# HGRN decay levels: split order on ScalarE and VectorE, query product ahead of the predicated copies, and the place of slab 12

## The chip, the cores and the metric

The kernel runs on one core of a Trainium2 chip. The metric is the device time of one execution in microseconds, the median of three. Both kernels compute the same thing on the same inputs.

## What is computed

A two-block model on 256 tokens with a model width of 1024, batch 1. The first block is a Mamba-2 mixer and a product-key expert layer; the second is an HGRN2 mixer, a gated convolutional FFN, windowed attention, and a second FFN. All of it is in float32. The part around the change is the HGRN2 mixer, which the reference writes by chunks of 32 tokens:

```python
def hgrn2_mixer(x, w_in, lower_bound, out_norm, w_out):
    q, f, i, g = jnp.split(x @ w_in, 4, axis=-1)
    q = jax.nn.silu(q) * HG_EXPAND ** -0.5
    forget = lower_bound + (1.0 - lower_bound) * jax.nn.sigmoid(f)
    logf = jnp.log(forget)
    k = 1.0 - forget
    o = hgrn2_chunked(heads(q), heads(k), heads(i), heads(logf))
    o = rms_norm(o, out_norm) * jax.nn.silu(heads(g))
    return o.reshape(b_, s_, D_MODEL) @ w_out
```

Inside `hgrn2_chunked` the score of a query t and an earlier key s is the sum over 128 features of q[t] k[s] exp(cum[t] - cum[s]), where cum is the running sum of logf. There are 8 heads.

## The kernel before

**Weights.** All weights pass through the core once, as a stream of 524 slabs of 128 x 1024 float32 (512 KB each), in a ring of 4 slots. SyncE loads a slab into `raw`. ScalarE copies it to `whi` (rounded to fp32r, the function `split_hi`, line 239), VectorE makes `wlo = raw - whi` (`split_lo`, line 247), and TensorE multiplies with both parts. A slab's `hi` waits until TensorE is done with the slab four places earlier in the ring (`slabs_done`), its `lo` waits for its `hi`, and the load of a slab waits for the `lo` of the slab four earlier.

**The HGRN stage.** Features f and q are projected first. Then 16 slabs, called 0 to 15 here, carry the projections of i and g, 12 matmuls of 512 columns each (`up_wide`, lines 326 to 328). Slabs 0 to 7 fill banks 0 to 3 with v, ScalarE copies these banks out (line 2098), and slabs 8 to 15 fill them again with the gate. In the text, "split k" is the pair `hi(k)`, `lo(k)` that prepares slab k+3: `hi(k)` may start once TensorE has finished slab k-1.

Between the slabs stand the nine *levels* that build the 256 x 256 decayed scores without ever forming an exponential that overflows. Level 8 is the diagonal, level 0 is the cross block between the two halves of the sequence, levels 1 to 7 have spans 64, 32 and so on down to 1. They run in the order 8, 0, 1, ..., 7. For a level x from 0 to 7:

- VectorE, `differences(x)`, here d(x): two subtractions of cum against the reference token of each block (lines 2180 and 2182).
- ScalarE, `level_exp(x)`, here e(x): two exponentials, query side and key side (lines 2063 and 2064). It waits for d(x).
- VectorE, `q_side(x)`, here q(x): the product of the query side with q (line 2217). It waits for the first half of e(x).
- TensorE, `level(x)`, here L(x): 16 float32 matmuls (8 for level 0) into banks 4 to 7; each shows as two records in the profile (line 1948; level 0 is line 1939). It waits for q(x), for e(x), and, bank by bank, for the take of the level before it.
- VectorE, `take(x)`, here t(x): four predicated copies, one per bank, that keep the level's own blocks (line 2233; for level 0 two plain copies, line 2226).

The buffers of d, e and q are two, so d(x) waits for L(x-2). After level 7 and slab 13 come the read-out (line 1970 on), slabs 14 and 15, the normalisation, the gate, and the output projection. Read-out waits for t(7).

**What sets the order.** No scheduler: each engine's queue is written out by hand, and each engine works its queue strictly as written. Two tables rule it, `LEVEL_ORDER` and `AFTER`, which says which slabs TensorE multiplies behind which level. ScalarE and VectorE derive the places of their splits from the same table. ScalarE's rule is the loop

```python
while done <= max(AFTER[x], default=0) + 1 and done < 14:
    slot_free(done)
    done += 1
if x + 2 < 8:
    level_exp(x + 2)
```

where `slot_free(k)` is `hi(k)`, with the four copies of v ahead of it for k = 8. So `hi` runs ahead of the exponentials of the same turn.

Of the kernel before, what the change touches and what calls it, by code (L numbers as in the profile page):

```python
# [131 lines left out]
def build(nc, t):  # L132
    ctx = ExitStack()
    with ctx:
# [21 lines left out]
        def V(name, i=0, n=1):  # L156
            o = VEC[name][0]
            if isinstance(i, int):
                return vec[:, o + i:o + i + n]
            return vec[:, bass.ds(i + o, n)]  # L160
# [36 lines left out]
        def s(name):  # L197

            if name not in S:
                S[name] = sem(name)  # L200
            return S[name]
# [31 lines left out]
        def split_hi(act, n0, i, r, U):  # L233
            if isinstance(i, int) and at(n0, i, r, U) >= N_SLABS:
                return
            q = slot(n0, r)
            act.wait_ge(raw_ready[q], (rounds(n0, i, r, U) + 1) * 16)
            act.wait_ge(slabs_done, at(n0, i, r, U) + 1)
            nc.scalar.activation(whi[:, q * 1024:(q + 1) * 1024], raw[:, q * 1024:(q + 1) * 1024],  # L239
                                 ACT.Copy).then_inc(hi_ready, 1)  # L240

        def split_lo(dve, n0, i, r, U):
            if isinstance(i, int) and at(n0, i, r, U) >= N_SLABS:
                return
            q = slot(n0, r)
            dve.wait_ge(hi_ready, at(n0, i, r, U) + 1)
            nc.vector.tensor_tensor(wlo[:, q * 1024:(q + 1) * 1024], raw[:, q * 1024:(q + 1) * 1024],  # L247
                                    whi[:, q * 1024:(q + 1) * 1024].bitcast(F32), ALU.subtract)\
                .then_inc(lo_ready, 1)
# [1656 lines left out]


        LEVEL_ORDER = (8, 0, 1, 2, 3, 4, 5, 6, 7)
        AFTER = {8: (2,), 0: (3,), 1: (4, 5), 2: (6, 7), 3: (8, 9), 4: (10,), 5: (11, 12), 6: (), 7: (13,)}
        PLACE_OF = {x: at for at, x in enumerate(LEVEL_ORDER)}  # L1910

        def span_of(x):
            return ((P,) + LEVELS[:-1])[x]

        def pe_hgrn(pe):
# [4 lines left out]
            def wide(k):  # L1920
                up_wide(pe, N_HG + 16 + k // 8 * 8, k % 8, s("v_out") if k == 8 else None)

            def level(x):

                before = LEVEL_ORDER[PLACE_OF[x] - 1] if PLACE_OF[x] else None
                if x < 8:
                    pe.wait_ge(s("qk_q"), x + 1)
                    pe.wait_ge(s("e_k"), x + 1)

                def bank_free(b):  # L1930
                    if before is not None:
                        pe.wait_ge(s("level_out"), 4 * PLACE_OF[x] - 4 + (4 if before == 0 else b + 1))

                qk = QK[x % 2]
                if x == 0:
                    for hd in range(HG_H):
                        if hd % 4 == 0:
                            bank_free(hd // 4)
                        nc.tensor.matmul(bank[4 + hd // 4][:, (hd % 4) * P:(hd % 4 + 1) * P],
                                         qk[:, hd * SEQ:hd * SEQ + P], qk[:, hd * SEQ + P:(hd + 1) * SEQ],  # L1940
                                         start=True, stop=True).then_inc(s("level_mm"), 2)
                    return
                for hc in range(2 * HG_H):
                    if hc % 4 == 0:
                        bank_free(hc // 4)
                    q = slice(hc * P, (hc + 1) * P)
                    a, b = (KK[:, q], QQ[:, q]) if x == 8 else (qk[:, q], qk[:, q])
                    nc.tensor.matmul(bank[4 + hc // 4][:, (hc % 4) * P:(hc % 4 + 1) * P], a, b,  # L1948
                                     start=True, stop=True).then_inc(s("level_mm"), 1)
# [8 lines left out]
            for x in LEVEL_ORDER:  # L1958
                level(x)
                for k in AFTER[x]:  # L1960
                    wide(k)
# [62 lines left out]
        def act_hgrn(act, chain):  # L2024
# [31 lines left out]
            def split(k):  # L2056
                split_hi(act, N_HG + 16 + k + AHEAD, 0, 0, 4)

            def level_exp(x):
                m = span_of(x)  # L2060
                act.wait_ge(s("dcum"), 2 * x + 2)
                e = QK[x % 2].rearrange("p (b w) -> p b w", w=2 * m)
                nc.scalar.activation(e[:, :, m:2 * m], e[:, :, m:2 * m], ACT.Exp).then_inc(s("e_q"), 1)
                nc.scalar.activation(e[:, :, 0:m], e[:, :, 0:m], ACT.Exp, scale=-1.0).then_inc(s("e_k"), 1)
# [29 lines left out]
            def slot_free(k):  # L2094
                if k == 8:
                    act.wait_ge(slabs_done, N_HG + 16 + 8 + RING)
                    for b in range(4):
                        nc.scalar.activation(VT[:, b * 512:(b + 1) * 512], bank[b][:, :], ACT.Copy)\
                            .then_inc(s("v_out"), 1)
                split(k)  # L2100
# [2 lines left out]
            split(0)  # L2103
            split(1)
            level_exp(1)
            done = 2
            for x in LEVEL_ORDER:
                while done <= max(AFTER[x], default=0) + 1 and done < 14:
                    slot_free(done)
                    done += 1  # L2110
                if x + 2 < 8:
                    level_exp(x + 2)
            split(14)
            nc.scalar.activation(tiny[:, 28:29], V("one"), ACT.Sqrt)
            squares(0)
            squares(1)
# [11 lines left out]
        def dve_hgrn(dve, chain):  # L2128
# [42 lines left out]
            def differences(x):  # L2171

                m = span_of(x)
                if x >= 2:
                    dve.wait_ge(s("level_mm"), 16 * (PLACE_OF[x - 2] + 1))
                e = QK[x % 2].rearrange("p (b w) -> p b w", w=2 * m)
                c3 = CUM.rearrange("p (b w) -> p b w", w=2 * m)
                k3 = CKN.rearrange("p (b w) -> p b w", w=2 * m)
                ref = c3[:, :, m - 1:m].to_broadcast([P, HG_H * SEQ // (2 * m), m])
                nc.vector.tensor_tensor(e[:, :, m:2 * m], c3[:, :, m:2 * m], ref, ALU.subtract)\  # L2180
                    .then_inc(s("dcum"), 1)
                nc.vector.tensor_tensor(e[:, :, 0:m], k3[:, :, 0:m], ref, ALU.subtract).then_inc(s("dcum"), 1)
# [26 lines left out]
            def split(k):  # L2209
                split_lo(dve, N_HG + 16 + k + AHEAD, 0, 0, 4)  # L2210

            def q_side(x):
                m = span_of(x)
                dve.wait_ge(s("e_q"), x + 1)
                e = QK[x % 2].rearrange("p (b w) -> p b w", w=2 * m)
                q3 = QQ.rearrange("p (b w) -> p b w", w=2 * m)
                nc.vector.tensor_tensor(e[:, :, m:2 * m], e[:, :, m:2 * m], q3[:, :, m:2 * m], ALU.mult)\
                    .then_inc(s("qk_q"), 1)

            def take(x):  # L2220

                at = PLACE_OF[x]
                if x == 0:
                    for b in range(2):
                        dve.wait_ge(s("level_mm"), 16 * at + 8 * (b + 1))
                        nc.vector.tensor_copy(CR[:, b * 512:(b + 1) * 512], bank[4 + b][:, :])\
                            .then_inc(s("level_out"), 2)
                    return
                for b in range(4):
                    dve.wait_ge(s("level_mm"), 16 * at + 4 * (b + 1))  # L2230
                    if at:
                        dve.wait_ge(s("level_out"), 4 * (at - 1) + b + 1)
                    nc.vector.copy_predicated(
                        PP[:, b * 512:(b + 1) * 512].rearrange("p (c t) -> p c t", t=P),
                        MASK[:, (x - 1) * P:x * P].bitcast(U32).unsqueeze(1).to_broadcast([P, 4, P]),
                        bank[4 + b][:, :].rearrange("p (c t) -> p c t", t=P)).then_inc(s("level_out"), 1)
# [6 lines left out]
            q_side(0)  # L2243
            split(1)
            for x in LEVEL_ORDER:
                if AFTER[x]:
                    split(AFTER[x][0])
                take(x)
                if x < 7:
                    q_side(x + 1)  # L2250
                if x + 2 < 8:
                    differences(x + 2)
                for k in AFTER[x][1:]:
                    split(k)
            split(14)

            def sums(half):
                for tt in range(TT):
# [461 lines left out]
        def act_block2(act, chain):  # L2720
            act_hgrn(act, chain)
            act_ffn(act, 0)
            act_attn(act, chain)
            act_ffn(act, 1)
            turn_act(act, T_OUT)
# [185 lines left out]
```

## Time and profile before

| what | value |
|---|---|
| median of 3 runs | 1718.12 us (1717.89 to 1719.43) |
| profiled execution | 1720.73 us |
| its span, first to last instruction | 1718.9 us |
| TensorE busy | 1672.3 us, 97% |
| VectorE busy | 1285.4 us, 75% |
| ScalarE busy | 1032.1 us, 60% |
| level stage, first level matmul to end of slab 13 | 1140.67 to 1209.36 us |

The span is what the trace covers; the profiled execution's own time has 1.83 us around it. Timeline rows give the start in microseconds from the span's start, the duration, engine, line, operation, output and input, and in brackets how long the engine sat idle before and which instruction released it. On VectorE and ScalarE a row's duration includes its tail, which overlaps the next instruction's start, so the step from start to start is what an instruction costs the queue.

### The profile page before, as it was taken

To read this page: it belongs to the slowest core of one execution; us is meant where nothing else is said; L and a number is where in the kernel's file an instruction comes from. 1 tells how busy PE (TensorE), PEld (TensorE's weight loads), DVE (VectorE), ACT (ScalarE), POOL (GpSimd) and SP (SyncE) were. 2 spreads that over 40 slices of the span, in tenths; PEclk is the share of its full clock that TensorE was granted. 3 is DMA by queue.
4 is the path that set the end of the run, shared out by engine and by line. 5 is a ranking of instruction groups with operands and counts; after the bars stand their busy time and mean duration, and the time that the engine had idled before them with its cause. 6 is when DMAs were issued, how large, how long until landed. Compare 5 with 4: busy or idle time off the path is not lost.

```text
span 1718.9 us, 34380 instructions
## 1 busy us (share of the span) xinstructions
PE 1672.3 (97%) x10835; PEld 1507.6 (88%) x10835; DVE 1285.4 (75%) x2361; ACT 1032.1 (60%) x1629; POOL 110.4 (6%) x101
## 2 busy tenths in 40 slices
PE   7999999999999999999999999999999998999998
PEld 6998889999999999988888888898888888778886
DVE  6876773799967777777777777789677777877776
ACT  7656554667556666655445445764576567666665
POOL 0014300344100000000000000100000000000000
PEclk9999999999999999999999999999999999999999
DMA  5543356577765555477787777543346554246563
GB/s 200 165 148 101 108 176 216 172 225 229 231 213 169 179 171 177 165 233 241 243 268 242 243 242 239 174 148 98 123 160 192 191 192 140 90 143 207 183 190 116
DMA packets 113261, 315.62 MB, mean 184 GB/s; under 512 B 12624, under 2 KB 44752, under 8 KB 112688
## 3 DMA queue, kind: packets, MB, share of 16 engines
q1 hardware_dynamic: 112352, 310.83, 55.9%
q0 software_dynamic: 848, 4.00, 0.7%
q8 instruction: 35, 0.57, 0.1%
q14 instruction: 26, 0.21, 0.0%
HBM read 296.43 MB, written 18.35 MB: 183 GB/s over the span
## 4 chain that ended last, share of the span: by engine, by line
PE 89%; DVE 5%; ACT 4%; issue 2%; DMA 1%; ACTq 0%; DVEq 0%; SPq 0%
PE bank L269 11%; PE bank L270 11%; PE bank L271 11%; PE bank L334 10%; PE bank L335 10%; PE bank L336 10%; PE bank L290 9%; PE bank L294 5%; PE bank L1496 3%; PE bank L1948 1%; DVE wlo L247 1%; ACT whi L239 1%; PE bank L326 1%; PE bank L328 1%; PE bank L327 1%
## 5 line engine op out<-in xcount | busy, mean ns | idle before, releaser
L247 DVE TENSOR_TENSOR wlo<-raw,whi 128x1024 fp32r<-128x1024 f32 x499 | 613.9, 1233 | 145.5 <-ACT whi L239 135.8
L239 ACT ACTIVATE whi<-raw 128x1024 fp32r<-128x1024 f32 x524 | 550.5, 1052 | 42.4 <-PE bank L328 36.0
L269 PE MATMUL bank<-x,whi 128*128 128x256 f32 (+1 forms) x1728 | 507.5, 294 | 5.2 <-DVE arena L897 1.7
L271 PE MATMUL bank<-x,wlo 128*128 128x256 f32 (+1 forms) x1728 | 491.7, 285 | 0.0
L270 PE MATMUL bank<-x,whi 128*128 128x256 f32 (+1 forms) x1728 | 491.4, 284 | 0.0
L269 PEld LDWEIGHTS bank<-x,whi 128*128 128x128 f32 x1728 | 331.3, 192 | 10.1 <-issue 8.1
L270 PEld LDWEIGHTS bank<-x,whi 128*128 128x128 f32 x1728 | 331.8, 192 | 0.1
L271 PEld LDWEIGHTS bank<-x,wlo 128*128 128x128 f32 x1728 | 331.0, 192 | 0.0
L334 PE MATMUL bank<-whi,yhi 128*128 128x512 f32 x816 | 319.5, 392 | 3.3 <-DVE ylo L716 1.9
L335 PE MATMUL bank<-wlo,yhi 128*128 128x512 f32 x816 | 318.2, 390 | 0.0
L336 PE MATMUL bank<-whi,ylo 128*128 128x512 f32 x816 | 317.7, 389 | 0.0
L334 PEld LDWEIGHTS bank<-whi,yhi 128*128 128x128 f32 x816 | 153.4, 188 | 36.1 <-issue 2.5
L336 PEld LDWEIGHTS bank<-whi,ylo 128*128 128x128 f32 x816 | 153.2, 188 | 32.5
L335 PEld LDWEIGHTS bank<-wlo,yhi 128*128 128x128 f32 x816 | 153.4, 188 | 29.5
L290 PE MATMUL bank<-x,whi 128*128 128x512 f32 x704 | 177.4, 392 | 0.9 <-DVE x L701 0.7
L1580 ACT ACTIVATE yhi<-h 128x256 fp32r<-128x256 f32 x128 | 53.4, 417 | 171.2 <-PE bank L336 167.2
L290 PEld LDWEIGHTS bank<-x,whi 128*128 128x128 f32 x704 | 129.3, 188 | 27.1 <-issue 1.1
L1533 ACT ACTIVATE h<-bank 128x256 f32<-128x256 f32 x128 | 49.1, 384 | 150.1 <-PE bank L271 149.9
L1774 DVE TENSOR_TENSOR ylo<-h,yhi 128x256 fp32r<-128x256 f32 x128 | 54.5, 425 | 66.2 <-ACT yhi L1580 66.2
L294 PEld LDWEIGHTS bank<-x,wlo 128*128 128x128 f32 x704 | 96.9, 190 | 6.9
L294 PE MATMUL bank<-x,wlo 128*128 128x256 f32 x704 | 100.2, 283 | 0.0
L1729 DVE TENSOR_SCALAR h<-iota,h 128x128 f32<-128x128 f32 x256 | 77.0, 344 | 22.8 <-PE bank L1496 22.8
(318 smaller groups left out, 1715.1 us busy)
## 6 DMA issues: line engine op xcount, KB each, us to landing
raw<-in_stream SPq DMA_DIRECT2D x524, 512.0 KB, 3.5
act_spill<-h SPq DMA_DIRECT2D x124, 128.0 KB, 3.2
h<-act_spill SPq DMA_DIRECT2D x124, 128.0 KB, 3.4
h<-in_x SPq DMA_DIRECT2D x1, 1024.0 KB, 5.2
arena<-in_keys POOLq DMA_DIRECT2D x1, 1024.0 KB, 6.0
h_spill<-h SPq DMA_DIRECT2D x1, 1024.0 KB, 8.7
arena<-h_spill POOLq DMA_DIRECT2D x1, 1024.0 KB, 7.4
arena<-in_g_final POOLq DMA_DIRECT2D x1, 512.0 KB, 9.3
```

What stands on the lines that cost most here:

```text
L239: nc.scalar.activation(whi[:, q * 1024:(q + 1) * 1024], raw[:, q * 1024:(q + 1) * 1024], ACT.Copy).then_inc(hi_ready, 1)
L247: nc.vector.tensor_tensor(wlo[:, q * 1024:(q + 1) * 1024], raw[:, q * 1024:(q + 1) * 1024], whi[:, q * 1024:(q + 1) * 1024].bitcast(F32), ...
L269: nc.tensor.matmul(bank[b][:, 0:T], whi[:, w], xhi[:, x], start=k == 0, stop=False)
L270: nc.tensor.matmul(bank[b][:, 0:T], whi[:, w], xlo[:, x], start=False, stop=False)
L271: last = nc.tensor.matmul(bank[b][:, 0:T], wlo[:, w], xhi[:, x], start=False, stop=k == KT - 1)
L290: return nc.tensor.matmul(bank[b][:, :], whi[:, w], both, start=k == 0, stop=k == KT - 1)
L294: return nc.tensor.matmul(bank[b][:, SEQ:2 * SEQ], wlo[:, w], xhi[:, k * SEQ:(k + 1) * SEQ], start=False, stop=stop, skip_group_check=True)
L334: nc.tensor.matmul(o, yhi[:, y], whi[:, w], start=first, stop=False, skip_group_check=True)
L335: nc.tensor.matmul(o, yhi[:, y], wlo[:, w], start=False, stop=False, skip_group_check=True)
L336: return nc.tensor.matmul(o, ylo[:, y], whi[:, w], start=False, stop=True, skip_group_check=True)
L1729: nc.vector.tensor_scalar(HOT1[:, y % 2 * P:(y % 2 + 1) * P], iota[:, :], c1(I1T), c1(GT_COLS), ALU.is_equal, ALU.mult).then_inc(s("hot_a" ...
L1774: nc.vector.tensor_tensor(ylo[:, yq * SEQ:(yq + 1) * SEQ], PRD[:, yq * SEQ:(yq + 1) * SEQ], yhi[:, yq * SEQ:(yq + 1) * SEQ].bitcast(F32), ...
```

## The change

Three tables now stand where one stood. `AFTER` moves slab 12 from behind level 5 to behind level 6. `HI_AT` gives ScalarE's `hi` places outright, and `LO_AT` gives VectorE's `lo` places. VectorE's q(x+1) now stands ahead of t(x). The last four `lo` (11 to 14) stand together after t(7).

```diff
--- before.py
+++ after.py
@@ -1906,7 +1906,9 @@
 
 
         LEVEL_ORDER = (8, 0, 1, 2, 3, 4, 5, 6, 7)
-        AFTER = {8: (2,), 0: (3,), 1: (4, 5), 2: (6, 7), 3: (8, 9), 4: (10,), 5: (11, 12), 6: (), 7: (13,)}
+        AFTER = {8: (2,), 0: (3,), 1: (4, 5), 2: (6, 7), 3: (8, 9), 4: (10,), 5: (11,), 6: (12,), 7: (13,)}
+        HI_AT = {8: (2,), 0: (3,), 1: (4,), 2: (5, 6), 3: (7, 8), 4: (9, 10), 5: (11,), 6: (12,), 7: (13, 14)}
+        LO_AT = {8: (2,), 0: (3,), 1: (4,), 2: (5, 6), 3: (7, 8), 4: (9,), 5: (10,), 6: (), 7: ()}
         PLACE_OF = {x: at for at, x in enumerate(LEVEL_ORDER)}
 
         def span_of(x):
@@ -2103,14 +2105,11 @@
             split(0)
             split(1)
             level_exp(1)
-            done = 2
             for x in LEVEL_ORDER:
-                while done <= max(AFTER[x], default=0) + 1 and done < 14:
-                    slot_free(done)
-                    done += 1
+                for k in HI_AT[x]:
+                    slot_free(k)
                 if x + 2 < 8:
                     level_exp(x + 2)
-            split(14)
             nc.scalar.activation(tiny[:, 28:29], V("one"), ACT.Sqrt)
             squares(0)
             squares(1)
@@ -2243,16 +2242,15 @@
             q_side(0)
             split(1)
             for x in LEVEL_ORDER:
-                if AFTER[x]:
-                    split(AFTER[x][0])
-                take(x)
+                for k in LO_AT[x]:
+                    split(k)
                 if x < 7:
                     q_side(x + 1)
+                take(x)
                 if x + 2 < 8:
                     differences(x + 2)
-                for k in AFTER[x][1:]:
-                    split(k)
-            split(14)
+            for k in (11, 12, 13, 14):
+                split(k)
 
             def sums(half):
                 for tt in range(TT):
```

**ScalarE, levels 8 to 1.** First the queue before, from `hi(2)` to e(3), then the queue after. `raw_ready2` is the load that `hi(2)` waits for, `raw_ready3` that of `hi(3)`, `raw_ready0` that of `hi(4)`, `raw_ready1` that of `hi(5)`. L2063 and L2064 are e(x) before; the same are L2065 and L2066 after.

```order
L239 ACTIVATE whi<-raw 128x1024 [waits slabs_done,raw_ready2]
L239 ACTIVATE whi<-raw 128x1024 [waits slabs_done,raw_ready3]
L239 ACTIVATE whi<-raw 128x1024 [waits slabs_done,raw_ready0]
L2063 ACTIVATE arena<-arena 128x32x32 [waits dcum]
L2064 ACTIVATE arena<-arena 128x32x32
L239 ACTIVATE whi<-raw 128x1024 [waits slabs_done,raw_ready1]
L239 ACTIVATE whi<-raw 128x1024 [waits slabs_done,raw_ready2]
L2063 ACTIVATE arena<-arena 128x64x16 [waits dcum]
L2064 ACTIVATE arena<-arena 128x64x16
```

```order
L239 ACTIVATE whi<-raw 128x1024 [waits slabs_done,raw_ready2]
L239 ACTIVATE whi<-raw 128x1024 [waits slabs_done,raw_ready3]
L2065 ACTIVATE arena<-arena 128x32x32 [waits dcum]
L2066 ACTIVATE arena<-arena 128x32x32
L239 ACTIVATE whi<-raw 128x1024 [waits slabs_done,raw_ready0]
L2065 ACTIVATE arena<-arena 128x64x16 [waits dcum]
L2066 ACTIVATE arena<-arena 128x64x16
L239 ACTIVATE whi<-raw 128x1024 [waits slabs_done,raw_ready1]
L239 ACTIVATE whi<-raw 128x1024 [waits slabs_done,raw_ready2]
```

`hi(4)` moved from ahead of e(2) to behind it, and `hi(5)` and `hi(6)` moved from ahead of e(3) to behind it.

**VectorE, levels 0 and 1.** From `lo(3)` to d(3). L247 is a `lo`, L2217 (L2216 after) is q(x), L2226 (L2225) and L2233 (L2232) are takes, L2180 and L2182 (L2179 and L2181) are d(x).

```order
L247 TENSOR_TENSOR wlo<-raw,whi 128x1024 [waits hi_ready]
L2226 COPY arena<-bank 128x512 [waits level_mm] x2
L2217 TENSOR_TENSOR arena<-arena 128x16x64 [waits e_q]
L2180 TENSOR_TENSOR arena<-arena 128x32x32 [waits level_mm]
L2182 TENSOR_TENSOR arena<-arena 128x32x32
L247 TENSOR_TENSOR wlo<-raw,whi 128x1024 [waits hi_ready]
L2233 COPY_PREDICATED arena<-arena,bank 128x512 [waits level_out,level_mm] x4
L2217 TENSOR_TENSOR arena<-arena 128x32x32 [waits e_q]
L2180 TENSOR_TENSOR arena<-arena 128x64x16 [waits level_mm]
L2182 TENSOR_TENSOR arena<-arena 128x64x16
```

```order
L247 TENSOR_TENSOR wlo<-raw,whi 128x1024 [waits hi_ready]
L2216 TENSOR_TENSOR arena<-arena 128x16x64 [waits e_q]
L2225 COPY arena<-bank 128x512 [waits level_mm] x2
L2179 TENSOR_TENSOR arena<-arena 128x32x32 [waits level_mm]
L2181 TENSOR_TENSOR arena<-arena 128x32x32
L247 TENSOR_TENSOR wlo<-raw,whi 128x1024 [waits hi_ready]
L2216 TENSOR_TENSOR arena<-arena 128x32x32 [waits e_q]
L2232 COPY_PREDICATED arena<-arena,bank 128x512 [waits level_out,level_mm] x4
L2179 TENSOR_TENSOR arena<-arena 128x64x16 [waits level_mm]
L2181 TENSOR_TENSOR arena<-arena 128x64x16
```

q(1) moved ahead of the takes of level 0, q(2) ahead of those of level 1. `lo(4)` keeps its place right behind d(2).

**TensorE, levels 6 and 7.** Before, the 32 instructions of both levels stand in one run; after, 16 of them are followed by the twelve matmuls of slab 12, and then come the other 16.

```order
L328 MATMUL bank<-whi,x 128x512
L1948 MATMUL bank<-arena 128x128 x32
L326 MATMUL bank<-whi,x 128x512
L327 MATMUL bank<-wlo,x 128x512
L328 MATMUL bank<-whi,x 128x512
L326 MATMUL bank<-whi,x 128x512
```

```order
L328 MATMUL bank<-whi,x 128x512
L1950 MATMUL bank<-arena 128x128 x16
L326 MATMUL bank<-whi,x 128x512
L327 MATMUL bank<-wlo,x 128x512
L328 MATMUL bank<-whi,x 128x512
L326 MATMUL bank<-whi,x 128x512
```

Between the two levels TensorE now has a slab's work, and behind level 5 it has one slab instead of two.

## Rows read from the trace of the kernel before

**Rows 1.** The page: busy engines, the chain that ended last, DMA issues.

```profile
PE 1672.3 (97%) x10835; PEld 1507.6 (88%) x10835; DVE 1285.4 (75%) x2361; ACT 1032.1 (60%) x1629; POOL 110.4 (6%) x101
...
PE 89%; DVE 5%; ACT 4%; issue 2%; DMA 1%; ACTq 0%; DVEq 0%; SPq 0%
...
raw<-in_stream SPq DMA_DIRECT2D x524, 512.0 KB, 3.5
```

**Rows 2.** Busy time, granted clock and DMA of 1150 to 1160 us.

```profile
core 0: us, PE busy (x) PEld busy (x) DVE busy (x) ACT busy (x) POOL busy (x), PEclk, DMA share, GB/s
1150.00:1160.00 10.00, 9.76 (x60) 8.37 (x59) 10.00 (x12) 4.13 (x4) 0.00 (x0) 1.00 0.34 105
```

**Rows 3.** Timeline of DVE, 1140 to 1211 us: start, duration, instruction, idle before.

```profile
1150.71 1.22 DVE L2217 TENSOR_TENSOR arena<-arena 128x1024 f32<-128x1024 f32 x1
1151.84 1.22 DVE L2180 TENSOR_TENSOR arena<-arena 128x1024 f32<-128x1024 f32 x1
1152.97 1.22 DVE L2182 TENSOR_TENSOR arena<-arena 128x1024 f32<-128x1024 f32 x1
1154.11 1.22 DVE L247 TENSOR_TENSOR wlo<-raw,whi 128x1024 fp32r<-128x1024 f32 x1
1155.24 2.61 DVE L2233 COPY_PREDICATED arena<-arena,bank 128x512 f32<-128x512 uint32 x4
1157.74 1.22 DVE L2217 TENSOR_TENSOR arena<-arena 128x1024 f32<-128x1024 f32 x1
...
1173.41 1.23 DVE L247 TENSOR_TENSOR wlo<-raw,whi 128x1024 fp32r<-128x1024 f32 x1 [2.69 <-ACT whi L239]
...
1210.71 1.23 DVE L247 TENSOR_TENSOR wlo<-raw,whi 128x1024 fp32r<-128x1024 f32 x1 [3.18 <-ACT whi L239]
```

**Rows 4.** Timeline of ACT, same stage.

```profile
1151.84 1.06 ACT L239 ACTIVATE whi<-raw 128x1024 fp32r<-128x1024 f32 x1 [3.50 <-PE bank L328]
1154.23 1.06 ACT L2063 ACTIVATE arena<-arena 128x1024 f32<-128x1024 f32 x1 [1.33 <-DVE arena L2182]
...
1170.38 2.06 ACT L2098 ACTIVATE arena<-bank 128x512 f32<-128x512 f32 x4 [1.60 <-PE bank L328]
1172.30 1.08 ACT L239 ACTIVATE whi<-raw 128x1024 fp32r<-128x1024 f32 x1
1173.25 1.08 ACT L2063 ACTIVATE arena<-arena 128x1024 f32<-128x1024 f32 x1
1174.20 1.08 ACT L2064 ACTIVATE arena<-arena 128x1024 f32<-128x1024 f32 x1
...
1209.62 1.06 ACT L239 ACTIVATE whi<-raw 128x1024 fp32r<-128x1024 f32 x1 [10.56 <-PE bank L328]
```

**Rows 5.** Timeline of PE, 1186 to 1210 us.

```profile
1186.49 3.84 PE L1948 MATMUL bank<-arena 128*128 128x128 f32 x32 [0.74 <-DVE arena L2217]
1190.09 0.48 PE L326 MATMUL bank<-whi,x 128*128 128x512 f32 x1
...
1195.63 3.73 PE L1948 MATMUL bank<-arena 128*128 128x128 f32 x32
1201.28 5.47 PE L1948 MATMUL bank<-arena 128*128 128x128 f32 x32 [1.92 <-DVE arena L2217]
1206.50 0.48 PE L326 MATMUL bank<-whi,x 128*128 128x512 f32 x1
...
1209.36 1.05 PE L1970 MATMUL bank<-arena 128*128 128x128 f32 x8
```

**Rows 6.** Granted clock of three single microseconds; columns as in rows 2.

```profile
1202.00:1203.00 1.00, 1.00 (x7) 1.00 (x6) 0.36 (x1) 0.00 (x0) 0.00 (x0) 0.50 0.00 0
1205.00:1206.00 1.00, 1.00 (x10) 1.00 (x10) 0.59 (x2) 0.00 (x0) 0.00 (x0) 0.94 0.20 78
1089.00:1090.00 1.00, 1.00 (x10) 1.00 (x9) 0.97 (x3) 0.98 (x4) 0.00 (x0) 0.97 0.00 0
```

**Rows 7.** Timeline of PE: two other idle gaps, elsewhere in the kernel.

```profile
1083.23 1.94 PE L668 MATMUL bank<-ident,arena 128*128 128x128 f32 x8 [3.17 <-DVE arena L515]
...
1461.41 1.01 PE L2506 MATMUL bank<-ident,arena 128*128 128x128 f32 x6 [1.75 <-DVE arena L2671]
```


## The prediction

> **What bounds the kernel now.** I began with the page. TensorE is busy for 97% of the span and holds 89% of the chain that ended last [rows 1], so the kernel is a queue of matmuls, and only what opens or closes a gap in that queue counts. The changed lines all work between 1140 and 1210 us. There the table by stretches is the second thing to read: from 1150 to 1160 us TensorE has 9.76 of 10 us and VectorE has 10.00 of 10 [rows 2]. Both are full, which is the warning of this case: a microsecond of waiting put into VectorE's queue has nowhere to go.
>
> Then the timelines. TensorE's shows where it loses time today: a gap of 0.74 us ahead of level 5 and one of 1.92 us ahead of level 7, both ended by q(x), and after the second gap level 7 takes 5.22 us from start to start where level 5 took 3.60 [rows 5]. In that stretch the granted clock is 0.50, that is 1.2 GHz instead of 2.4, and it is back in the microsecond after 1205 [rows 6]. Idle gaps of 3.17 and 1.75 us elsewhere [rows 7] show that the longer one is followed by half clock until about 1089.06 [rows 6]. So about 4 us of this stage could be won (1.92 + 0.74 idle, 1.62 of half clock), and the change aims there.
>
> VectorE's timeline gives the steps, start to start: 1.13 us for q, for a `lo` and for each half of d, and 2.50 us for a take [rows 3]. It also shows what happens when a `lo` comes before its `hi`: 2.69 us of idle ahead of `lo(8)` [rows 3], because on ScalarE the `hi(8)` stood behind the four copies of v, which took 1.92 us of its queue [rows 4]. ScalarE's steps are 0.95 us for a `hi` and for each exponential; a `hi` ends 1.06 us after its start, and a waiting instruction starts about 0.04 us after what releases it (`lo(8)` at 1173.41 after `hi(8)`'s end at 1173.38) [rows 3, 4].
>
> **The change part by part.**
>
> *q(x+1) ahead of t(x).* The operations stay the same. It hides 2.50 us of takes behind the next level's first matmuls, since that level then needs only the first bank's take. Cover: the bank-by-bank waits. It removes both gaps in principle.
>
> *Slab 12 between levels 6 and 7.* No operation is added; TensorE's work is moved. Alone it fills the 1.92 us gap with 2.86 us of slab work (1206.50 to 1209.36 is one slab behind a level) [rows 5].
>
> *`hi` behind the exponentials.* This is the part with a price. Before, `hi(4)` ran at 1151.84, while VectorE was still making d(2); e(2) followed at 1154.23, the moment d(2) ended [rows 4], and `lo(4)` ran at 1154.11 without a wait [rows 3]. Now ScalarE's queue has e(2) first, and e(2) waits for d(2). VectorE's next instruction behind d(2) is still `lo(4)`, which needs `hi(4)`. So VectorE stands idle through a full round: d(2) ends, e(2) takes 1.91 us, `hi(4)` takes 1.06, and 0.07 goes to handing over. It is the same for d(3) and `lo(5)`, d(4) and `lo(7)`, d(5) and `lo(9)`. What is queued behind the waiting `lo`: the next q, which TensorE's next level needs, and the take and d behind it, which the next e needs. The loop closes on itself, so the idle time adds up from level to level.
>
> *The replay*, from the start of d(2), 1151.84, which does not move (q(1) and t(0) only swap):
> - d(3) starts 2.39 (d and its handover) + 1.91 (e) + 1.10 (`hi`) + 1.13 (`lo`) + 1.13 (q) + 2.50 (take) = 10.16 us later, 1162.0. One level before needed 7.0 (2.27 + 1.13 + 2.50 + 1.13).
> - d(4): the same with a second `lo`, 11.29 us, 1173.3.
> - d(5): on ScalarE e(4), `hi(7)` 0.95, the copies 1.92, `hi(8)` 1.10, then on VectorE `lo(8)`, q(4), t(3): 13.0 us, 1186.3. TensorE cannot start slab 8 before the first copy of v is out, at 1179.15, and idles about 4.0 us behind level 3, which ends at 1175.1.
> - d(6): 10.16 us, 1196.5. Level 5 waits for q(5) and the first bank of t(4), until 1194.7, a gap of 3.7 us or, if slab 8 ran at half clock, of about 2.
> - d(7): `hi(10)` is long done, so no idle time: 7.03 us, 1203.5.
> - q(7) waits for the first half of e(7): 3.5 us, 1207.05. t(6) starts at 1208.2, its first bank is free at 1208.95, and level 7 starts at 1209.0. Before it was 1201.28.
> - Level 7 takes 3.60 now, at full clock, and slab 13 2.86: it ends at 1215.5, against 1209.36 before [rows 5].
>
> The same ledger on the order of before, with its own waits, comes within about 0.2 us of the rows. Sum: **+6.1 us** (7.7 us late at level 7, less 1.6 us of half clock that is no longer paid there).
>
> *The four late `lo`.* `lo(11)` to `lo(13)` start when t(7) ends, about 1213.6, and take 3.4 us, until 1217.0; `lo(14)` needs `hi(14)`, which starts when slab 13 is done, about 1215.7, and ends at 1216.8. Cover: ScalarE's table load, and squares that keep the first sum of VectorE away until about 3.35 us behind slab 13, 1218.8; in the old order `lo(14)` ran 1.35 us behind slab 13 [rows 3, 5]. Cost nothing, with 0.6 us of cover left. Slabs 14 and 15 are needed only after the read-out. The loads wait for these `lo` too: the load for `hi(15)` starts near 1214.8 and takes 3.5 us [rows 1], and `hi(15)` comes some 10 us behind slab 13. Cost nothing.
>
> *Clock.* The rows show half clock after gaps of 1.92 and 3.17 us and none after 1.75 [rows 5 to 7]; it cost 1.6 and (1089.06 - 1083.23)/2 = 2.9 us. The change makes a gap of 4.0 us ahead of slab 8 and one of 2 to 3.7 ahead of level 5. The loss behind the first is hidden, since level 4 and its slab are through before q(5). The loss behind the second reaches level 7 only in part: with 1.6 us it starts at 1209.2 instead of 1209.0, with 2.9 at 1210.4. I take 0.1 and keep 0 to 1.4. The Trainium skill ("TensorE: Matmul & The Clock Gate", Part 1) says that an idle TensorE falls to the lower clock and that sustained activity gives the upper one back; by it every long gap here is charged anew, and the sum would be at the upper end of that bound. The trace agrees for two gaps.
>
> **Sum.** The profiled execution took 1720.73 us for a span of 1718.9; with +6.1 it would be 1726.8. It stands 2.6 above the median of the runs, so the median becomes 1718.12 + 6.1 = **1724.2 us**. About 0.2%, 3.4 us, is what a measurement of this kernel can tell from no change.
>
> **The rivals.**
> - *The intended gain.* If `hi` were never late, TensorE would have no gap: from 1151.98 seven levels at about 3.5 and ten slabs, seven at 2.86 and three at 2.7, end at 1204.6, 4.8 us earlier: 1713.3 us. It decides if ScalarE can run `hi(4)` while e(2) still waits. For it: TensorE's waits for q are real. Against it: `hi(8)` waited behind the copies, and the order shows e(2) ahead of `hi(4)`. The Trainium skill (the same page, the table at its head) calls ScalarE's queue strictly first in, first out; by that rule this rival falls. Chance 0.08.
> - *The clock on top.* Half clock behind the gap of level 5 costs 2.9, and the timed runs of before have less half clock than the profiled one, so that the 1.6 is not won back: +6.1 + 1.2 + 1.6 = 8.9 at most, 1727.0. For it: the profiled run is the slowest seen. Chance 0.14.
> - *No change to be told.* The idle time is paid in fewer rounds than I count, two of four: with 3.1 us for a round, +6.1 becomes about 0. For it: VectorE has slack behind level 7 (3.18 us idle [rows 3]). Against it: that slack is behind the last q. Chance 0.05.
> - The forecast, 0.73, has its own range of 1722.3 to 1726.0.
>
> **Numbers.** Slower by over 0.2% is the forecast and the clock case, 0.87; faster 0.08; same 0.05. The range, 1721.9 to 1727.4, leaves out the intended gain, the no-change case and the tip of the clock case.
>
> **What would show it.** In the changed kernel's timeline: VectorE idle 3.1 us ahead of `lo(4)`, `lo(5)`, `lo(9)` and more ahead of `lo(7)` and `lo(8)` together, ended by ScalarE's line 239; e(2) at 1154.2 and `hi(4)` at 1156.1; a TensorE gap of about 4 us ahead of slab 8; level 7 near 1209; read-out near 1215.5. It is wrong if `lo(4)` starts near 1154.1, or if the read-out starts before 1210, and incomplete if the tail behind slab 13 is longer than before.

## The result and the profile after

| | before | changed |
|---|---|---|
| median of 7 runs each | 1719.43 us (1717.89 to 1720.80) | 1724.59 us (1723.09 to 1726.48) |
| profiled execution, its span | 1720.73, 1718.9 us | 1723.52, 1721.7 us |
| level stage, first level matmul to read-out | 68.69 us | 74.77 us |
| the span without the stage | 1650.2 us | 1646.9 us |

The changed kernel is slower by 5.2 us, a ratio of 1.0033 with a 95% interval of 1.0024 to 1.0042. Its time lies 0.4 us above the forecast of 1724.2. The forecast had started from the first three runs of before, whose median was 1718.12; against the seven the difference is 5.2 us where 6.1 were forecast. The stage itself grew by 74.77 - 68.69 = 6.08 us. What lies outside the stage is 3.3 us shorter in this pair of profiled executions, 2.65 us of it ahead of the stage, where nothing was changed; the last section comes back to it.

The timelines of the changed kernel begin 2.65 us earlier at this place, so times are read against the first level matmul: 1140.67 before, 1138.02 now. First ScalarE and VectorE at levels 0 to 3, in the changed kernel (L2065 is the first half of e, L239 a `hi`, L2100 the copies of v; L247 a `lo`, L2216 q, L2232 a take, L2179 and L2181 are d). The timeline of ACT:

```profile
1151.58 1.06 ACT L2065 ACTIVATE arena<-arena 128x1024 f32<-128x1024 f32 x1 [5.89 <-DVE arena L2181]
1152.54 1.04 ACT L2066 ACTIVATE arena<-arena 128x1024 f32<-128x1024 f32 x1
1153.49 1.04 ACT L239 ACTIVATE whi<-raw 128x1024 fp32r<-128x1024 f32 x1
1161.70 1.06 ACT L2065 ACTIVATE arena<-arena 128x1024 f32<-128x1024 f32 x1 [7.17 <-DVE arena L2181]
...
1174.83 1.04 ACT L239 ACTIVATE whi<-raw 128x1024 fp32r<-128x1024 f32 x1
1175.78 2.04 ACT L2100 ACTIVATE arena<-bank 128x512 f32<-128x512 f32 x4
1177.68 1.07 ACT L239 ACTIVATE whi<-raw 128x1024 fp32r<-128x1024 f32 x1
```

The timeline of DVE:

```profile
1150.32 1.22 DVE L2181 TENSOR_TENSOR arena<-arena 128x1024 f32<-128x1024 f32 x1
1154.56 1.23 DVE L247 TENSOR_TENSOR wlo<-raw,whi 128x1024 fp32r<-128x1024 f32 x1 [3.02 <-ACT whi L239]
1155.70 1.22 DVE L2216 TENSOR_TENSOR arena<-arena 128x1024 f32<-128x1024 f32 x1
...
1164.69 2.36 DVE L247 TENSOR_TENSOR wlo<-raw,whi 128x1024 fp32r<-128x1024 f32 x2 [3.02 <-ACT whi L239]
...
1175.90 1.22 DVE L247 TENSOR_TENSOR wlo<-raw,whi 128x1024 fp32r<-128x1024 f32 x1 [3.01 <-ACT whi L239]
1178.79 1.23 DVE L247 TENSOR_TENSOR wlo<-raw,whi 128x1024 fp32r<-128x1024 f32 x1 [1.66 <-ACT whi L239]
...
1188.91 1.23 DVE L247 TENSOR_TENSOR wlo<-raw,whi 128x1024 fp32r<-128x1024 f32 x1 [3.02 <-ACT whi L239]
...
1204.38 1.23 DVE L2216 TENSOR_TENSOR arena<-arena 128x1024 f32<-128x1024 f32 x1 [1.21 <-ACT arena L2065]
...
1210.88 4.62 DVE L247 TENSOR_TENSOR wlo<-raw,whi 128x1024 fp32r<-128x1024 f32 x4
1216.14 1.28 DVE L2259 TENSOR_REDUCE arena<-arena 128x4 f32<-128x512 f32 x2 [0.64 <-ACT arena L2072]
```

Where `lo(4)` followed d(2) at once before, at 1154.11 [rows 3], VectorE now sits idle for 3.02 us. The chain can be read off the two fences: d(2)'s second half starts at 1150.32 and ends at 1151.54, e(2) starts at 1151.58, the `hi` at 1153.49, and the `lo` at 1154.56. On ScalarE, `hi(4)` had been ready to run since slab 3 ended; before, it ran while ScalarE had nothing else to do, with 3.50 us of idle time ahead of it and 1.33 us behind it [rows 4]. The same 3.02 us stand ahead of `lo(5)` (1164.69), 3.01 ahead of `lo(7)` (1175.90) and 3.02 ahead of `lo(9)` (1188.91). `lo(8)` waits another 1.66 us, since its `hi` stands behind the copies of v.

TensorE's timeline, changed kernel:

```profile
1138.02 3.73 PE L1950 MATMUL bank<-arena 128*128 128x128 f32 x32
...
1168.97 3.81 PE L1950 MATMUL bank<-arena 128*128 128x128 f32 x32 [1.20 <-DVE arena L2232]
...
1176.50 0.76 PE L326 MATMUL bank<-whi,x 128*128 128x512 f32 x1 [3.72 <-ACT arena L2100]
...
1192.06 3.81 PE L1950 MATMUL bank<-arena 128*128 128x128 f32 x32 [0.97 <-DVE arena L2232]
...
1199.22 3.81 PE L1950 MATMUL bank<-arena 128*128 128x128 f32 x32 [0.60 <-DVE arena L2232]
...
1206.40 3.81 PE L1950 MATMUL bank<-arena 128*128 128x128 f32 x32 [0.59 <-DVE arena L2232]
1209.97 0.48 PE L326 MATMUL bank<-whi,x 128*128 128x512 f32 x1
...
1212.79 1.05 PE L1972 MATMUL bank<-arena 128*128 128x128 f32 x8
```

The gap that the prediction expected ahead of slab 8 is there, 3.72 us, ended by the copies of v. The table by stretches shows the clock behind it:

```profile
1176.00:1179.00 3.00, 2.50 (x6) 2.05 (x7) 1.34 (x2) 2.76 (x5) 0.00 (x0) 0.50 0.24 72
1179.00:1181.00 2.00, 2.00 (x6) 1.52 (x6) 2.00 (x2) 0.00 (x0) 0.00 (x0) 0.50 0.38 154
```

Half clock (1.2 GHz), and 2 us of TensorE with 6 matmuls. Level 7 takes 3.57 us, 1206.40 to 1209.97, and slab 13 the next 2.82 us; before, level 7 took 5.22 us at half clock [rows 5]. The lists of waits from 1138 to 1220 us, first before, then changed. Columns: who waited on whom, us in total, times, longest.

```profile
DVE wlo L247 <- ACT whi L239: 7.0, 3, 3.2
...
PE bank L1948 <- DVE arena L2217: 2.9, 3, 1.9
```

```profile
DVE wlo L247 <- ACT whi L239: 14.8, 6, 3.0
...
PE bank L326 <- ACT arena L2100: 3.7, 1, 3.7
PE bank L1950 <- DVE arena L2232: 3.4, 4, 1.2
```

TensorE's matmuls now wait no longer for q, but for the first bank of a take and for v. VectorE's wait for ScalarE has doubled from 7.0 to 14.8 us. Of the 7.0 us, 3.18 stand behind slab 13 [rows 3]; inside the stage it grew from 3.8 to 14.8 us.

### The profile page after: what moved, and what is told of

Read it like the earlier page. It is cut to its first block, busy times and chain, and to the rows that moved or that the text cites. A ratio compares the mean times of both kernels' runs of the same rounds, so it can differ in the third digit from the quotient of the medians.

```text
span 1721.7 us, 34380 instructions
## 1 busy us (share of the span) xinstructions
PE 1671.6 (97%) x10835; PEld 1505.6 (87%) x10835; DVE 1283.7 (75%) x2361; ACT 1031.1 (60%) x1629; POOL 111.8 (6%) x101
## 3 DMA queue, kind: packets, MB, share of 16 engines
q1 hardware_dynamic: 112352, 310.83, 55.6%
## 4 chain that ended last, share of the span: by engine, by line
PE 86%; DVE 6%; ACT 4%; issue 2%; DMA 1%; ACTq 0%; DVEq 0%; SPq 0%
PE bank L269 11%; PE bank L270 11%; PE bank L271 11%; PE bank L334 10%; PE bank L335 10%; PE bank L336 10%; PE bank L290 9%; PE bank L294 5%; PE bank L1496 3%; DVE arena L2232 1%; ACT whi L239 1%; DVE wlo L247 1%; DVE arena L897 1%; PE bank L1467 0%; PE bank L1950 0%
## 5 line engine op out<-in xcount | busy, mean ns | idle before, releaser
L247 DVE TENSOR_TENSOR wlo<-raw,whi 128x1024 fp32r<-128x1024 f32 x499 | 613.2, 1232 | 152.8 <-ACT whi L239 143.2
L239 ACT ACTIVATE whi<-raw 128x1024 fp32r<-128x1024 f32 x524 | 550.3, 1052 | 16.3 <-PE bank L328 9.9
```

## The experiments

The theory is the prediction's: the whole loss is the round d, e, `hi`, `lo` in which VectorE stands idle, once for each level, and the other two parts of the change are gains. For each run, "stage" is first level matmul to read-out in its profile. The runs came in three batches, each on a chip of its own with its own runs of before.

| kernel | median, us | before in its batch | ratio, 95% | stage, us | span less stage |
|---|---|---|---|---|---|
| changed, `hi` ahead of e | 1715.02 | 1719.04 | 0.9967 to 0.9985 | 64.06 | 1649.6 |
| before, new `hi` places | 1735.84 | 1719.04 | 1.0092 to 1.0123 | 86.02 | 1646.5 |
| before, q ahead | 1715.85 | 1719.04 | 0.9975 to 0.9993 | 64.96 | 1648.0 |
| before, slab 12 moved | 1717.36 | 1719.04 | 0.9983 to 1.0001 | 66.36 | 1647.2 |
| before, q ahead and slab 12 | 1714.81 | 1719.17 | 0.9966 to 0.9987 | 64.95 | 1647.5 |
| changed, one round back | 1722.28 | 1719.17 | 1.0011 to 1.0029 | 71.81 | 1649.6 |
| before, new `lo` places | 1717.76 | 1719.17 | 0.9984 to 1.0002 | 67.72 | 1648.3 |
| changed, takes first | 1727.88 | 1719.17 | 1.0036 to 1.0063 | 76.52 | 1649.6 |
| changed, round of v back | 1720.72 | 1719.57 | 1.0000 to 1.0018 | 69.92 | 1648.8 |
| changed, again | 1723.78 | 1719.57 | 1.0016 to 1.0037 | 74.82 | 1649.1 |
| changed, takes first, again | 1727.21 | 1719.57 | 1.0026 to 1.0054 | 77.46 | 1649.9 |
| changed, `hi` ahead of e, again | 1714.82 | 1719.57 | 0.9960 to 0.9981 | 64.02 | 1649.7 |

### The `hi` ahead of the exponentials again

```diff
-        HI_AT = {8: (2,), 0: (3,), 1: (4,), 2: (5, 6), 3: (7, 8), 4: (9, 10), 5: (11,), 6: (12,), 7: (13, 14)}
+        HI_AT = {8: (2, 3), 0: (4,), 1: (5, 6), 2: (7, 8), 3: (9, 10), 4: (11,), 5: (12,), 6: (13,), 7: (14,)}
```

> The changed kernel with one thing put back: on ScalarE every hi stands ahead of the exponentials again (hi(4) ahead of e(2), hi(5) and hi(6) ahead of e(3), and so on). Theory (the loss is the round d, e, hi, lo that VectorE waits through): the idle time ahead of lo(4), lo(5), lo(7), lo(9) goes, and so do TensorE's gap ahead of slab 8 and the half clock behind it. The stage from level 8 to the read-out takes about 63.8 us instead of 74.8 in the changed kernel and 68.7 in the kernel before, so the whole is about 4.5 to 5 us faster than before (1714.5 by the 7-run median of before, 1719.4). Rival A (the loss is q ahead of the takes or the late lo, ScalarE's order is innocent): it stays within 1.5 us of the changed kernel, about 1724. Rival B (the gain of the other parts is not there): level with before, 1719.

Measured: 1715.02 us, 4.0 below before and about 9.6 below the changed kernel, which was timed in another batch. The stage is 64.06 where 63.8 was expected, and the gain is a little under the expected 4.5 to 5. One table on one engine turns the loss into a gain. The timeline of DVE in this kernel, at d(2) and behind it:

```profile
1152.77 1.22 DVE L2181 TENSOR_TENSOR arena<-arena 128x1024 f32<-128x1024 f32 x1
1153.91 1.22 DVE L247 TENSOR_TENSOR wlo<-raw,whi 128x1024 fp32r<-128x1024 f32 x1
1155.12 1.23 DVE L2216 TENSOR_TENSOR arena<-arena 128x1024 f32<-128x1024 f32 x1
...
1161.00 2.58 DVE L247 TENSOR_TENSOR wlo<-raw,whi 128x1024 fp32r<-128x1024 f32 x2
...
1173.31 1.23 DVE L247 TENSOR_TENSOR wlo<-raw,whi 128x1024 fp32r<-128x1024 f32 x1 [2.71 <-ACT whi L239]
```

`lo(4)` follows d(2) at 1153.91 with no idle time; the only long wait left is the 2.71 us ahead of `lo(8)`, which before had too [rows 3]. This kernel's row in the table by stretches for the whole stage, then that of the changed kernel:

```profile
1140.47:1204.53 64.06, 63.73 (x417) 57.32 (x416) 58.56 (x67) 28.33 (x30) 0.00 (x0) 1.00 0.31 100
```

```profile
1138.02:1212.79 74.77, 67.35 (x418) 58.93 (x416) 58.47 (x67) 27.35 (x30) 0.00 (x0) 0.95 0.26 85
```

TensorE is busy for 63.73 of 64.06 us at full clock. By this profile only 0.33 us of the stage is not its work. Rivals A and B both fall.

> The changed kernel with every hi ahead of the exponentials, again, for the best version: 4 to 5 us below before and 10 to 11 us below the changed kernel in this batch, stage 64.1 us.

Measured: 1714.82, 4.75 below before in its batch and 9.0 below the changed kernel, stage 64.02. The stage difference is 10.8, the medians give 9.0 and the means of the runs 9.9: slightly under the 10 to 11 expected, with the same stage.

### ScalarE's new order on the kernel before

```diff
-                while done <= max(AFTER[x], default=0) + 1 and done < 14:
-                    slot_free(done)
-                    done += 1
+                for k in HI_AT[x]:
+                    slot_free(k)
```

> The kernel before with ScalarE's new order alone (the new hi places; VectorE and TensorE as before). Theory: the same loss in a purer form, and larger, because VectorE's old order puts a lo ahead of every take and a second one behind d: ledger about 83.9 to 86.8 us for the stage instead of 68.7, so 1735 to 1737. Rival A (ScalarE's order is innocent): 1719 to 1720.

Measured: 1735.84, 16.8 us above before, stage 86.02. The part that loses does so by itself, and the old order of VectorE makes it worse. Its list of waits:

```profile
DVE wlo L247 <- ACT whi L239: 21.2, 8, 3.2
...
PE bank L1949 <- DVE arena L2215: 14.5, 6, 5.4
```

VectorE waits 21.2 us for `hi`, in 8 places, where before it was 3.8 us in 2 places of the stage. TensorE waits 14.5 us for q.

### q ahead of the takes alone

```diff
-                take(x)
                 if x < 7:
                     q_side(x + 1)
+                take(x)
```

> The kernel before with q(x+1) ahead of t(x) alone. Theory: this part is the gain; both TensorE gaps (0.74 and 1.92 us) and the half clock behind the second go, the stage takes about 64.5 us instead of 68.7, the whole about 4 us less than before, 1715.2. t(7) ends later against the end of slab 13 (0.9 us ahead of it instead of 1.9) without being felt. Rival (the takes ahead of the matmuls cost nothing, since the clock or the bank waits hold TensorE anyway): 1718.5 to 1719.5.

Measured: 1715.85, 3.2 below before, stage 64.96. TensorE's gap ahead of level 5 is gone and that ahead of level 7 is 0.76 us, and level 7 runs at full clock. The expectation had both gaps gone and a stage of 64.5; this 0.76 us is what it missed:

```profile
1184.01 3.73 PE L1948 MATMUL bank<-arena 128*128 128x128 f32 x32
...
1197.57 3.81 PE L1948 MATMUL bank<-arena 128*128 128x128 f32 x32 [0.76 <-DVE arena L2233]
```

### Slab 12 behind level 6 alone, and both

```diff
-        AFTER = {8: (2,), 0: (3,), 1: (4, 5), 2: (6, 7), 3: (8, 9), 4: (10,), 5: (11, 12), 6: (), 7: (13,)}
+        AFTER = {8: (2,), 0: (3,), 1: (4, 5), 2: (6, 7), 3: (8, 9), 4: (10,), 5: (11,), 6: (12,), 7: (13,)}
```

> The kernel before with slab 12 moved behind level 6 alone (the splits follow by the old rules). Theory: it covers the 1.92 us gap ahead of level 7 and keeps the clock up, but leaves a gap ahead of level 6 of some 0.6 to 1.5 us, too short to bring half clock: stage about 66.2 us, the whole about 2.3 to 2.6 us less than before, 1717. Rival (the half clock comes anyway, behind another gap): within 0.7 us of before.

Measured: 1717.36, 1.7 below before instead of 2.3 to 2.6, with an interval that just touches no change; the gain is seen in the stage, 66.36, which is 2.33 less. Levels 5, 6 and 7 each wait (0.74, 0.46, 0.45 us) and none of them runs at half clock; level 7:

```profile
1197.77 3.84 PE L1948 MATMUL bank<-arena 128*128 128x128 f32 x32 [0.45 <-DVE arena L2217]
```

> The kernel before with q ahead of the takes and slab 12 behind level 6; the splits keep the old rules. Theory: once q is ahead, TensorE has no gap left ahead of level 7 that slab 12 could fill, so the second part adds nothing to the first: stage 64.5 us as with q alone, the whole about 1715.5. Rival (the parts add up): 64.5 less the 2.5 us that slab 12 won alone, that is about 1713.

Measured: stage 64.95 against 64.96 for q ahead alone. The two parts don't add up, since both fill the same gap. The median, 1714.81, is 1.0 below that of q alone, but in another batch.

### One round put back

```diff
-        HI_AT = {8: (2,), 0: (3,), 1: (4,), 2: (5, 6), 3: (7, 8), 4: (9, 10), 5: (11,), 6: (12,), 7: (13, 14)}
+        HI_AT = {8: (2,), 0: (3,), 1: (4, 5, 6), 2: (), 3: (7, 8), 4: (9, 10), 5: (11,), 6: (12,), 7: (13, 14)}
```

> The changed kernel with hi(5) and hi(6) alone put back ahead of e(3). Theory (each round of d, e, hi, lo is paid once, and they add up): exactly one round of 3.0 us goes, VectorE no longer idles ahead of lo(5), and everything later moves with it: stage about 71.8 us instead of 74.8, the whole about 1721.5. Rival (the rounds don't add up, the longest one or the copies of v set the time): stage within 1 us of 74.8, about 1724.5.

Measured: stage 71.81 instead of 74.77, that is 2.96 less, and a median of 1722.28. The timeline of DVE in this kernel has the idle time ahead of `lo(4)` still, and none ahead of `lo(5)`:

```profile
1157.12 1.23 DVE L247 TENSOR_TENSOR wlo<-raw,whi 128x1024 fp32r<-128x1024 f32 x1 [3.02 <-ACT whi L239]
...
1164.14 2.36 DVE L247 TENSOR_TENSOR wlo<-raw,whi 128x1024 fp32r<-128x1024 f32 x2
```

This round alone costs 3.0 us.

### The round of v put back

```diff
-        HI_AT = {8: (2,), 0: (3,), 1: (4,), 2: (5, 6), 3: (7, 8), 4: (9, 10), 5: (11,), 6: (12,), 7: (13, 14)}
+        HI_AT = {8: (2,), 0: (3,), 1: (4,), 2: (5, 6, 7, 8), 3: (), 4: (9, 10), 5: (11,), 6: (12,), 7: (13, 14)}
```

> The changed kernel with hi(7), the four copies of v and hi(8) put back ahead of e(4), nothing else. Theory: TensorE's gap ahead of slab 8 goes with its half clock, and so does the longest idle round of VectorE (3.0 + 1.7 us ahead of lo(7) and lo(8)): stage 69.9 to 71.2 us instead of 74.8, the whole about 1720. Rival (the 3.7 us gap and the half clock are hidden, and this round is like the others): stage 71.8, as when hi(5) and hi(6) alone went back, 1722.

Measured: stage 69.92, 4.9 less than the changed kernel of the same batch, as the theory had it, with the copies of v on ScalarE. The median, 1720.72, is only 3.1 us less, and the means of the runs differ by 3.7.

The rounds don't simply add up. Three rounds of 2.96 us and this one of 4.9 would make 13.8 us, but with every `hi` put back the stage is 10.8 us shorter. VectorE's waits for `hi` account for that: 14.8 us in the changed kernel's stage, 3.8 us (1.06 and 2.71) with every `hi` ahead of e. The 2.71 us ahead of `lo(8)` come back once VectorE is no longer late; with the round of v alone put back there is no wait ahead of `lo(8)`.

### The new places of `lo` alone

```diff
-                if AFTER[x]:
-                    split(AFTER[x][0])
+                for k in LO_AT[x]:
+                    split(k)
                 take(x)
...
-                for k in AFTER[x][1:]:
-                    split(k)
-            split(14)
+            for k in (11, 12, 13, 14):
+                split(k)
```

> The kernel before with VectorE's new places of lo alone (takes still ahead of q; ScalarE and TensorE as before). Theory: slightly faster, since no lo stands behind level 5 and 6 between a take and q(7) that need not be there: stage about 67.5 us, 1.0 to 1.2 less than before, 1718; the four late lo are hidden behind t(7). Rival (they push the sums, so the tail behind slab 13 gets longer): 1719.5 to 1721.

Measured: 1717.76, stage 67.72, 0.97 less than before, again with an interval that touches no change. The gain is the expected one, but not at the expected place: 0.88 of it is there when level 5 starts (44.94 us behind the first level matmul instead of 45.82), since one `lo` fewer stands ahead of q(5). The gap ahead of level 7 and its half clock stay. The take of level 6, which q(7) stands behind, waits 1.13 us for the matmuls of level 6; VectorE's row, then TensorE's:

```profile
1194.33 3.40 DVE L2234 COPY_PREDICATED arena<-arena,bank 128x512 f32<-128x512 uint32 x4 [1.13 <-PE bank L1949]
```

```profile
1198.90 5.46 PE L1949 MATMUL bank<-arena 128*128 128x128 f32 x32 [1.92 <-DVE arena L2218]
```

The four late `lo` cost nothing. That is also seen in the changed kernel: they start at 1210.88, take 4.6 us, and VectorE is idle for 0.64 us ahead of the first sum. This sum starts at 1216.14, 3.35 us behind slab 13, as in the kernel before:

```profile
1212.71 1.28 DVE L2261 TENSOR_REDUCE arena<-arena 128x4 f32<-128x512 f32 x2 [0.77 <-ACT arena L2070]
```

### The takes first in the changed kernel

```diff
-                if x < 7:
-                    q_side(x + 1)
                 take(x)
+                if x < 7:
+                    q_side(x + 1)
```

> The changed kernel with the takes ahead of q again. Theory: q ahead is worth less here than alone, since VectorE's idle rounds set the time of d and both orders cost VectorE the same; only level 7's start gains: stage 75.8 to 78 us instead of 74.8, the whole 1725.5 to 1727.5. Rival (q ahead is worth its 3 to 4 us here too): 1728 or more.

Measured: 1727.88, 0.1 below the rival's line and 0.4 above the theory's, while the stage, 76.52, says 1.7 us. So both kernels were run again, in one batch.

> The changed kernel again, on the chip of its companions: 1724 to 1725, stage 74.8 us. It is here so that the next run can be compared with it on one chip.

> The changed kernel with the takes ahead of q, again. Theory (q ahead is worth 1.7 us here, as the stages of the two profiles say: 76.5 against 74.8): 1.2 to 2.2 us above the changed kernel in this batch. Rival (it is worth 3 us or more, as the medians of two batches say: 1727.9 against 1724.6): 2.8 us or more above it.

Measured: 1723.78 for the changed kernel (stage 74.82), and 1727.21 with the takes first (stage 77.46). The medians differ by 3.4 us, which is the rival's number; the means of the same runs differ by 2.5 us and the stages by 2.6. All three lie above the 1.2 to 2.2 of the theory. With 8 and 5 runs that spread over 3.3 and 3.7 us, the runs don't tell 2.5 from 3.4, so the rival's 2.8 or more is not shown. The two profiles with the takes first differ in level 5, behind a gap of 3.46 us in both:

```profile
1196.20 5.47 PE L1950 MATMUL bank<-arena 128*128 128x128 f32 x32 [3.46 <-DVE arena L2216]
```

```profile
1196.21 6.43 PE L1950 MATMUL bank<-arena 128*128 128x128 f32 x32 [3.46 <-DVE arena L2216]
```

5.47 us in one and 6.43 in the other: the same gap costs a different amount of half clock from one execution to the next. The 1.7 us had been read from one profile of each kernel, and such a reading moves by about 1 us from pair to pair.

## Why the prediction was right

- **Program order against the waits.** The step that carried it, `hi(4)` behind e(2) behind d(2), is shown by the 3.02 us, and by the run that puts the `hi` back: stage 64.06, where the rival "intended gain" had worked out 4.8 us less than before, 63.9. The run of before with the new `hi` places alone shows the loss without the other parts of the change.
- **The sum.** +6.1 for the stage, measured 6.08, and 6.13 with the second profile of the changed kernel. By levels from the first level matmul, forecast and measured: d(3) 21.3 and 21.3, d(4) 32.6 and 32.5, d(5) 45.6 and 45.5, d(6) 55.8 and 55.6, d(7) 62.8 and 62.8, level 7 68.3 and 68.4. Its terms were start-to-start steps of single rows, not means. The 1.6 us of half clock that it took back were won: level 7 took 3.57 us. One round was put at 3.1 us and measured 3.02.
- **What was mis-sized.** The gap ahead of level 5 was put at about 2 to 3.7 us with half clock behind it. It was 0.97 us in the first profile, with level 5 at full clock, since slab 8's half clock had taken the time before it; in the second profile of the same kernel it was 2.14 us, and level 5 took its half clock there. The stage is 74.77 and 74.82: the forecast that this loss would be nearly hidden held both ways, and the bound of 1.4 us was not needed.
- **The base.** The forecast stood on a median of three, 1718.12; seven gave 1719.43. So 1724.2 came closer to 1724.59 than the difference did (5.2 and, in the later batch, 4.2 us, for 6.1). That is partly luck: a base 1.3 us too low and a difference 0.9 us too high nearly cancel. The intervals, 4.1 to 7.2 us and 2.8 to 6.4 us, both hold 6.1. In single executions the span without the stage varies by 3.7 us; that the missing 0.9 and 1.9 us are what is left of this between medians of 7 or 8 runs is likely, not shown.
- **The rivals.** The clock on top: not needed. Half clock came behind the gap ahead of slab 8 in both profiles of the changed kernel, and behind the gap of level 5 in the second, where it was hidden. The intended gain: real for q ahead and slab 12, but not in this kernel. No change to be told: excluded, since all four waits of 3.0 us are in the profile and two of the rounds were each taken out by a run of their own.

## What to carry to other kernels

When a hand-written order is loosened on one engine, write down for each moved instruction which engine's next instruction it now stands behind. `hi` runs in time that ScalarE spends waiting; putting it behind an instruction that waits for VectorE made VectorE wait for its own result to come round. A gain (q ahead, 3.7 us of stage) and a loss (10.8 us) can sit in one diff: take them apart before judging either. The shortest stage here is that of the change with its `HI_AT` set back, 4.0 to 4.8 us faster than before. The kernel before with q ahead and slab 12 moved alone is 4.4 us faster; its stage is 0.9 us longer, which is what the new `lo` places are worth, and the medians don't tell the two apart.

## What was not expected

**The same gap, with and without half clock.** I had taken the gap's length as a guide, from 1.92 us (half clock) and 1.75 us (none). With the takes first, level 3 came behind a gap of 1.94 us in the first profile and of 1.91 us in the second:

```profile
1173.12 3.84 PE L1950 MATMUL bank<-arena 128*128 128x128 f32 x32 [1.94 <-DVE arena L2216]
```

```profile
1173.15 5.46 PE L1950 MATMUL bank<-arena 128*128 128x128 f32 x32 [1.91 <-DVE arena L2216]
```

The level behind the longer gap ran at full clock, the one behind the shorter gap mostly at half clock. In the first profile the clock then fell in slab 8, behind another gap of 1.99 us. Level 5 with the round of v back came behind 2.64 us, at full clock; its row, and that of the table by stretches:

```profile
1188.64 3.81 PE L1950 MATMUL bank<-arena 128*128 128x128 f32 x32 [2.64 <-DVE arena L2232]
...
1188.00:1192.00 4.00, 3.36 (x30) 3.39 (x31) 4.00 (x6) 0.00 (x0) 0.00 (x0) 1.00 0.35 126
```

3.73 to 3.84 us for a level is full clock, 5.44 to 6.43 is not. In the level stage of these traces all seven gaps from 3.46 to 5.42 us were followed by half clock, none up to 1.49 us was, and of the ten from 1.91 to 2.64 us five were. The Trainium skill ("TensorE: Matmul & The Clock Gate", Part 1) says of its warm-up that it varies from run to run; the fall does too, by these rows.

**Half clock with a busy TensorE.** In some executions, and not in others, TensorE's clock falls around 100 us or 130 us, where nothing was changed. Before, then the changed kernel:

```profile
100.00:105.00 5.00, 5.00 (x35) 4.93 (x35) 4.79 (x13) 3.35 (x7) 0.00 (x0) 0.74 0.48 151
```

```profile
100.00:105.00 5.00, 5.00 (x45) 4.91 (x44) 4.76 (x16) 3.76 (x7) 0.00 (x0) 1.00 0.65 191
```

TensorE is busy for 5.00 of 5 us in both, with 35 and 45 matmuls. The only gap ahead of it is of 0.83 us, and around 130 us there is none: there TensorE is busy for 10.00 of 10 us from 127 to 137 in every profile. What both places have in common is what TensorE did just before: matmuls that use 24 or 16 of the 128 rows. The row of before at 97.09 us, and, from the first run with the takes first, the matmuls at 126.22 us with the clock behind them:

```profile
97.09 0.67 PE L1112 MATMUL bank<-arena 24*96 24x256 f32 x2
```

```profile
126.22 3.22 PE L1152 MATMUL bank<-arena 16*128 16x384 f32 x8
...
130.00:132.00 2.00, 2.00 (x11) 2.00 (x11) 0.00 (x0) 0.91 (x1) 1.96 (x1) 0.50 0.00 0
```

These matmuls stand there in every execution, whether the clock falls or not, so they are at most one condition; no run took them away. Of the fourteen profiled executions four have no fall at either place, six have one and four have both. Their level stage starts at 1137.4 to 1138.5, at 1139.0 to 1140.7 and at 1140.5 to 1140.7 us, and the span without the stage is 1646.5 to 1647.5, 1648.0 to 1650.2 and 1649.6 to 1649.9 us. So these falls go with most of the spread, and a pair of profiles can show 2.8 us where the stage moved by 6.1. What decides when the clock falls there was not tried.
